# A four-block transformer on one core: softmax scaling moved from VectorE to GpSimd, and decay rows in two row groups

## The chip, the cores and the metric

One core of a Trainium2 chip. The time is device microseconds of one execution, the median of three runs; lower is better. Everything is in float32. TensorE's granted clock has two levels, 2.4 and 1.2 GHz; the profile gives it as a share of the higher one (PEclk).

## What is computed

A sequence of 256 tokens, 1024 wide, goes through a first block (an HGRN/RG-LRU mixer and a feed-forward; then a forgetting attention, "fox", and a feed-forward) and a second block (latent attention, "mla", and a feed-forward; then an S5 state-space mixer and a mixture of eight experts). The change lies in the two attentions, cut here to what matters:

```
def fox_attention(q, k, v, f_logit):                    # 16 heads of 64
    c = cumsum(log_sigmoid(f_logit), axis=1)            # one decay row of 256 per head
    for blk in range(2):                                # query blocks of 128
        logits = einsum('bhqd,bhkd->bhqk', q[blk] * 64**-0.5, k[:end])
        logits = logits + c[q] - c[k]
        p = softmax(where(causal, logits, -inf))
        out[blk] = einsum('bhqk,bhkd->bhqd', p, v[:end])

def mla_mixer(...):                                     # 16 heads of 64, and 32 rotary dimensions
    s = einsum(q_nope, k_nope) + einsum(q_pe, k_pe)
    p = softmax(where(causal, s * scale, NEG_INF))
    o = einsum(p, v)
```

The term `c[q]` is the same for a whole softmax row and falls out, so the kernel adds only `-c[k]`.

## The kernel before, in words

Each engine has a program of its own, in a fixed order written out by hand; the engines meet at semaphores. Both attentions run through `attention(kind, ...)`, which exists once for TensorE (L1309), once for ScalarE (L641) and once for VectorE (L1983). The 16 heads go in 8 pairs. A head has 384 columns of scores in one PSUM bank: query block 0 against keys 0 to 127, then query block 1 against keys 0 to 255. Banks 4 to 7 hold two pairs.

For pair p, TensorE does, in this order:

- `scores(p + 2)`: the products q·k of two heads (`head_products`, L1377; a head has 64 partitions, 0 to 63 or 64 to 127); then in mla the rotary products (L1458; 32 partitions, at 32 times the head's number modulo 4), and in fox the decay rows (L1422: a column of the identity, broadcast, times `negc`, 16 partitions by 384 columns, one matmul per head); then the causal mask (L1332). A float32 matmul stands in the profile as two.
- `output(p - 1)`: probabilities times values (L1353).
- `turn(2p)`, `turn(2p + 1)`: six transposes of probabilities (L1341). Each head's wait for `at["prob"]`.

ScalarE takes the exponentials with their row sums (L649, L652), writes the mask into a freed bank (`biased`, L659), copies the turned probabilities of the even head to SBUF (L667) and the pair's output (L672).

VectorE takes the maxima (`maximum`, L1989 to L1993), copies the odd head's turned probabilities (`turned`, L2009), and normalizes (`normalize`, L1995): a reciprocal of the two row sums (L1998), then the two scalings of `pbuf` in place, 128 and 256 columns (L1999, L2001). Its order in the loop over pairs is

```
maximum(2 * p + 2)
maximum(2 * p + 3)
if p:
    turned(p - 1)
normalize(2 * p)
normalize(2 * p + 1)
```

so that in the last two pairs, which have no maxima left, a reciprocal and its scalings come straight after a copy. `negc` is made once, in VectorE's `fox` (L2050 on), from `cum`, on partitions 0 to 15.

GpSimd has two memsets at the start (L506, L507), a causal select in the first mixer (L510), and the three pieces of `mask3` (L515, L516), which it writes at 130 us. After that its program is at its end.

Of the kernel before, what the change touches and what calls it, by code (L numbers as in the profile page):

```python
# [14 lines left out]
P = 128  # L15
T = 256
# [149 lines left out]
def build_program(nc, a):  # L166

    ctx = ExitStack()
    with ctx:
# [86 lines left out]
        def pair(f, k):  # L256
# [38 lines left out]
            "rate", "conv", "product", "gates", "decay", "square", "root")}  # L295
        at = {n: sem("at_" + n) for n in (
            "flog", "maskmade", "biased", "fscaled", "rcol", "rcoltaken", "fbias", "logsig", "c", "vtile", "vtaken", "scores", "max", "exp", "prob",
            "pturned", "eventaken", "oddtaken", "out", "posrow", "poscol", "reduced", "trig", "turned", "roped")}
        s5 = {n: sem("s5_" + n) for n in (
            "dt", "angle", "mag", "trig", "bbar", "bturned", "btaken", "steps", "phase", "sincos",  # L300
            "astep", "cstep", "kcopied", "kernel", "aturned", "ataken", "bu", "rotated", "state", "y", "ysum", "z")}
# [65 lines left out]
        UP0, SCALED0, HID0 = ({name: m * FT0[name] for name in LATE} for m in (2, 1, 1))  # L367

        cum, fz, fa = (scr[0:HEADS, i * T:(i + 1) * T] for i in range(3))
        negc = scr[0:HEADS, 4 * T:4 * T + 3 * P]  # L370
        mraw = part(0, 6).rearrange("p (a n) -> p a n", a=6)
        mnorm = part(6, 5).rearrange("p (a n) -> p a n", a=5)
        qpe_raw = part(12, 4).rearrange("p (a n) -> p a n", a=4)
# [130 lines left out]
        @block.gpsimd  # L504
        def _(pool):
            pool.memset(ones[:, :], 1.0).then_inc(cleared, 1)  # L506
            pool.memset(xbp[:, :, 0:3], 0.0).then_inc(cleared, 1)  # L507

            pool.wait_ge(hg["scopied"], 2)
            pool.affine_select(out=sc, in_=sc, pattern=[[0, 16], [1, CHUNK]], base=0,  # L510
                               channel_multiplier=-1, compare_op=ALU.is_ge, fill=0.0
                               ).then_inc(hg["masked"], 1)
            pool.wait_ge(mix_ready, KD)
            for b in (0, 2):
                pool.tensor_copy(mask3[:, b * P:(b + 1) * P], mask).then_inc(at["maskmade"], 1)  # L515
            pool.memset(mask3[:, P:2 * P], 0.0).then_inc(at["maskmade"], 1)  # L516


        @block.scalar
# [486 lines left out]
        def _(pe):  # L1006
# [310 lines left out]
            def attention(kind, products):  # L1317
                n0 = at0[kind]
                p0 = n0 // 2
                b0 = 0 if kind == "fox" else HEADS // 2 - 2  # L1320

                def scores(p):

                    if p >= 2:
                        pe.wait_ge(at["biased"], b0 + p - 1)
                        pe.wait_ge(at["exp"], n0 + 2 * p - 2)
                    else:
                        pe.matmul(ps[:, 4 + 2 * p, 0:3 * P], ident, mask3, start=True, stop=False,
                                  skip_group_check=True)
                    products((2 * p, 2 * p + 1))  # L1330
                    for c in (0, 2 * P):
                        m = pe.matmul(ps[:, 5 + 2 * p % 4, c:c + P], ident, mask, start=False,  # L1332
                                      stop=True, skip_group_check=True)
                    m.then_inc(at["scores"], 1)

                def turn(h):
                    pe.wait_ge(at["prob"], n0 + h + 1)
                    if h >= 2:
                        pe.wait_ge(at[("eventaken", "oddtaken")[h % 2]], p0 + h // 2)
                    for b in range(3):  # L1340
                        m = pe.transpose(ps[:, 2 + h % 2, b * P:(b + 1) * P],  # L1341
                                         pbuf[h % 4][:, b * P:(b + 1) * P], ident)
                    m.then_inc(at["pturned"], 1)

                def output(p):

                    pe.wait_ge(at["eventaken"], p0 + p + 1)
                    pe.wait_ge(at["oddtaken"], p0 + p + 1)
                    if p >= 2:
                        pe.wait_ge(mix_ready, mix_at[kind] + p - 1)  # L1350
                    for b in range(2):
                        for h in (2 * p, 2 * p + 1):
                            m = pe.matmul(ps[HD * (h % 2):HD * (h % 2) + HD, p % 2, b * P:T],  # L1353
                                          vtok[:, b, h * HD:(h + 1) * HD],
                                          pTs[h % 4][:, 2 * b * P:2 * P + b * P], start=b == 0,
                                          stop=b == 1, skip_group_check=True)
                    m.then_inc(at["out"], 1)

                pe.wait_ge(at["vtaken"], 4 if kind == "fox" else 8)
                pe.wait_ge(at["maskmade"], 3)  # L1360
                scores(0)
                scores(1)
                for p in range(HEADS // 2):
                    if p + 2 < HEADS // 2:
                        scores(p + 2)
                    if p:
                        output(p - 1)
                    turn(2 * p)
                    turn(2 * p + 1)
                output(HEADS // 2 - 1)  # L1370
# [28 lines left out]
            def fox():  # L1399
                linear("odd_qk", hT, h_ready, H0["n4"], range(1))  # L1400
                for c in range(KD):
                    m = pe.matmul(acc(2)[0:HEADS], wf[:, c, :], hT[:, c], start=c == 0,
                                  stop=c == KD - 1, skip_group_check=True)
                m.then_inc(at["flog"], 1)
                presummed_total("n4")
                linear("odd_qk", hT, h_ready, H0["n4"], range(1, 3))
                pe.wait_ge(rstd_ready, NORM_NO["n4"] + 1)
                for g in range(2):
                    pe.matmul(ps[:, 0, g:g + 1], rstd[0:1, g * P:(g + 1) * P], ones[0:1, 0:1],
                              start=True, stop=True, skip_group_check=True).then_inc(at["rcol"], 1)  # L1410
                linear("odd_qk", hT, h_ready, H0["n4"], range(3, 16))
                pe.wait_ge(at["fscaled"], 1)
                pe.wait_ge(at["rcoltaken"], 1)
                values("odd_v", hT, KD, 0)
                pe.wait_ge(tile_taken, TILE0["odd_qk"] + 16)
                pe.wait_ge(at["c"], 2)

                def products(heads):
                    head_products(heads)
                    for h in heads:  # L1420
                        one = cst[0:HEADS, CST["ident"] + h:CST["ident"] + h + 1]
                        m = pe.matmul(ps[:, 4 + h % 4, 0:3 * P], one.to_broadcast([HEADS, P]), negc,  # L1422
                                      start=False, stop=h % 2 == 0, skip_group_check=True)
                        if h % 2 == 0:
                            m.then_inc(at["scores"], 1)

                attention("fox", products)

            def mla():
# [3 lines left out]
                busy(2, 3)  # L1433
                total("mq")

                pe.wait_ge(at["posrow"], 2)
                pe.matmul(acc(2), onesrow, posf, start=True, stop=True, skip_group_check=True
                          ).then_inc(at["poscol"], 1)
                total("mkv", 3)
                busy(6, 3)  # L1440
                linear("mla_uq", mnorm, h_ready, H0["mq"])
# [391 lines left out]
        def _(dve):  # L1833
# [149 lines left out]
            def attention(kind):  # L1983
# [9 lines left out]
                    dve.tensor_scalar(stat[:, h, 3:5], stat[:, h, 0:2], -scale_of[kind], None,  # L1993
                                      ALU.mult).then_inc(at["max"], 1)

                def normalize(h):
                    dve.wait_ge(at["exp"], n0 + h + 1)
                    step(dve.reciprocal(stat[:, h, 7:9], stat[:, h, 5:7]))  # L1998
                    dve.tensor_scalar(pbuf[h % 4][:, 0:P], pbuf[h % 4][:, 0:P], stat[:, h, 7:8],  # L1999
                                      None, ALU.mult)  # L2000
                    dve.tensor_scalar(pbuf[h % 4][:, P:3 * P], pbuf[h % 4][:, P:3 * P],  # L2001
                                      stat[:, h, 8:9], None, ALU.mult).then_inc(at["prob"], 1)

                def turned(p):

# [8 lines left out]
                for p in range(HEADS // 2):  # L2014
                    if p + 1 < HEADS // 2:
                        maximum(2 * p + 2)
                        maximum(2 * p + 3)
                    if p:
                        turned(p - 1)
                    normalize(2 * p)  # L2020
                    normalize(2 * p + 1)
                turned(HEADS // 2 - 1)

            def fox():
# [13 lines left out]
                for i in range(1, 3):  # L2038
# [8 lines left out]
                dve.tensor_tensor_scan(cum, one.to_broadcast([HEADS, T]), fz, 0.0, ALU.mult, ALU.add  # L2047
                                       ).then_inc(at["c"], 1)
                dve.wait_ge(at["c"], 1)
                dve.tensor_scalar(negc[:, 0:P], cum[:, 0:P], -1.0, None, ALU.mult)  # L2050
                dve.tensor_scalar(negc[:, P:3 * P], cum, -1.0, None, ALU.mult
                                  ).then_inc(at["c"], 1)
                for i in range(4, 16):
                    take_tile(i)
                attention("fox")
# [242 lines left out]
            def mla():  # L2298
# [6 lines left out]
                                      ).then_inc(tile_taken, 1)  # L2305
                dve.wait_ge(tile_taken, TILE0["mla_in"] + 6)
                dve.wait_ge(late_loaded, 16 * 4)
                dve.tensor_copy(posf, pos_i[:, :]).then_inc(at["posrow"], 1)
                dve.memset(onesrow, 1.0).then_inc(at["posrow"], 1)
                pre_norm("mq", mraw, mnorm, "q_norm", 0)  # L2310

                dve.wait_ge(at["poscol"], 1)
                step(dve.tensor_scalar(ang, acc(2), v("inv_freq", 0), None, ALU.mult))
                reduce_angle(red, ang, turns).then_inc(at["reduced"], 1)
                pre_norm("mkv", mraw[:, 3:5], mnorm[:, 3:5], "kv_norm", 0)
# [467 lines left out]
```

## Time and profile before

| | |
|---|---|
| three runs | 2281.67, 2281.91, 2285.21 us; median 2281.91 |
| profiled execution, span | 2281.3 us; the page gives no other time of that execution |
| busy in the span | TensorE 2211.3 us (97%), VectorE 871.5 (38%), ScalarE 467.1 (20%), GpSimd 3.3 (0%) |
| mean granted clock | 0.989 |
| fox attention | 489.88 to 530.46 us |
| mla attention | 864.01 to 900.52 us |

Times in the rows are microseconds from the start of the span. Busy time is the time in which an engine executed something; instructions of one engine overlap in part, so a row's length is not its share of the engine, and start-to-start distances are the safer reading. A matmul's end is modelled.

### The profile page before, as it was taken

The numbers are of one execution on the slowest core, as the hardware profiler recorded it, in microseconds if no ns is written. First come the engines' busy times: TensorE is split into PE (matmuls) and PEld (weight loads), VectorE is DVE, ScalarE is ACT, GpSimd is POOL, SyncE is SP. The second block draws the span as 40 slices with busy tenths as digits, with TensorE's granted clock in tenths as the row PEclk, the third lists the DMA queues.
The fourth block names the chain that finished last, engine by engine and source line by source line (L and its number), as shares of the span: only waits on it lengthen the run. The fifth ranks groups of instructions, "written<-read, shape, count | busy, mean of one in ns | idle before, by whom it ended". The sixth has DMA issues, their size and how long they took to land.

```text
span 2281.3 us, 67869 instructions
## 1 busy us (share of the span) xinstructions
PE 2211.3 (97%) x30612; PEld 2019.5 (89%) x30612; DVE 871.5 (38%) x2198; ACT 467.1 (20%) x1074; POOL 3.3 (0%) x10
## 2 busy tenths in 40 slices
PE   9999999999999999999978999999999999999998
PEld 8879998857899876999966899999999999999998
DVE  4257765224766536567678210101010101111101
ACT  3432112123211234110043211111111111111111
POOL 0000000000000000000000000000000000000000
PEclk9999999999999999999999999999999999999999
DMA  7142444232144322444322199999999999999996
GB/s 322 74 166 96 155 159 164 92 129 111 70 160 160 134 81 105 190 158 158 119 98 93 56 337 398 330 399 343 393 339 391 353 368 374 359 381 344 390 355 253
DMA packets 103298, 522.45 MB, mean 229 GB/s; under 512 B 8402, under 2 KB 8531, under 8 KB 95443
## 3 DMA queue, kind: packets, MB, share of 16 engines
q1 hardware_dynamic: 103122, 519.82, 59.3%
q8 instruction: 146, 2.39, 0.4%
q14 instruction: 30, 0.24, 0.0%
HBM read 518.74 MB, written 1.05 MB: 228 GB/s over the span
## 4 chain that ended last, share of the span: by engine, by line
PE 61%; DVE 3%; ACT 1%; issue 1%; DVEq 0%; ACTq 0%
PE ps L1731 26%; PE ps L1745 13%; PE ps L1126 6%; PE ps L1159 4%; PE ps L1056 3%; PE ps L1521 2%; PE ps L1718 1%; PE ps L1689 1%; DVE scr L2393 1%; PE ps L1703 0%; PE ps L1391 0%; PE ps L1377 0%; PE ps L1458 0%; PE ps L1504 0%; PE ps L1353 0%
## 5 line engine op out<-in xcount | busy, mean ns | idle before, releaser
L1731 PE MATMUL ps<-scr,slot 128*64 128x96 f32 x14336 | 636.6, 246 | 2.8 <-issue 2.7
L1731 PEld LDWEIGHTS ps<-scr,slot 128*64 128x64 f32 x14336 | 610.9, 137 | 4.0 <-issue 3.7
L1745 PE MATMUL ps<-scr,slot 128*64 128x96 f32 x7168 | 341.3, 247 | 0.0
L1745 PEld LDWEIGHTS ps<-scr,slot 128*64 128x64 f32 x7168 | 313.3, 137 | 24.0 <-issue 24.0
L2522 DVE TENSOR_TENSOR scr<-scr,ps 128x96 f32<-128x96 f32 x224 | 56.5, 252 | 611.8 <-PE ps L1731 611.8
L1159 PE MATMUL ps<-scr,slot 128*128 128x256 f32 x1056 | 244.7, 387 | 7.9 <-DVE scr L2210 7.9
L1159 PEld LDWEIGHTS ps<-scr,slot 128*128 128x128 f32 x1056 | 200.3, 195 | 34.9 <-DVE scr L2210 9.5
L908 ACT ACTIVATE scr<-ps 128x96 f32<-128x96 f32 x224 | 56.1, 250 | 824.9 <-PE ps L1731 824.9
L1126 PE MATMUL ps<-vtok,slot 128*128 128x128 f32 x1056 | 139.8, 276 | 2.7 <-DVE vtok L2150 2.7
L1126 PEld LDWEIGHTS ps<-vtok,slot 128*128 128x128 f32 x1056 | 128.6, 192 | 3.5 <-DVE vtok L2150 3.5
L1126 PE MATMUL ps<-vtok,proj 128*128 128x128 f32 x1056 | 128.7, 275 | 0.0
L1126 PEld LDWEIGHTS ps<-vtok,proj 128*128 128x128 f32 x1056 | 123.2, 192 | 0.0
L1126 PEld LDWEIGHTS ps<-hT,slot 128*128 128x128 f32 x960 | 116.4, 192 | 2.9
L1126 PE MATMUL ps<-hT,slot 128*128 128x128 f32 x960 | 116.9, 275 | 0.0
L1056 PE MATMUL ps<-hT,slot 128*128 128x256 f32 x480 | 111.1, 385 | 3.9 <-issue 1.6
L1056 PEld LDWEIGHTS ps<-hT,slot 128*128 128x128 f32 x480 | 89.1, 190 | 23.4 <-issue 6.7
L2136 DVE TENSOR_TENSOR proj<-slot 128x512 f32<-128x512 f32 x132 | 91.1, 690 | 6.2 <-ACT mixT L672 2.9
L765 ACT ACTIVATE sq<-ps 128x128 f32<-128x128 f32 x66 | 18.3, 277 | 364.4 <-PE ps L1126 364.4
L1208 PE MATMUL ps<-hT,slot 128*128 128x256 f32 x384 | 89.5, 394 | 2.2 <-DMA slot<-in_w_even_in 1.9
L1208 PEld LDWEIGHTS ps<-hT,slot 128*128 128x128 f32 x384 | 75.5, 198 | 14.3 <-DMA slot<-in_w_even_in 2.1
L2160 DVE TENSOR_TENSOR sq<-sq,ps 128x128 f32<-128x128 f32 x66 | 18.9, 287 | 175.4 <-ACT sq L765 175.4
L1056 PE MATMUL ps<-mixT,slot 128*128 128x256 f32 x384 | 84.6, 381 | 1.3 <-PE ps L1056 0.9
(391 smaller groups left out, 2127.3 us busy)
## 6 DMA issues: line engine op xcount, KB each, us to landing
slot<-in_w_moe SPq DMA_DIRECT2D x224, 1024.0 KB, 7.1
slot<-in_w_moe SPq DMA_DIRECT2D x224, 512.0 KB, 6.9
slot<-in_w_ffn SPq DMA_DIRECT2D x33, 3072.0 KB, 10.2
slot<-in_w_even_in SPq DMA_DIRECT2D x3, 3072.0 KB, 27.4
slot<-in_w_odd_qk SPq DMA_DIRECT2D x2, 3072.0 KB, 10.9
slot<-in_w_s_glu SPq DMA_DIRECT2D x2, 3072.0 KB, 11.3
slot<-in_w_odd_v SPq DMA_DIRECT2D x2, 2048.0 KB, 8.2
slot<-in_w_even_in SPq DMA_DIRECT2D x2, 1536.0 KB, 11.8
```

Of the source, the lines that this page charges most:

```text
L908: act.activation(gbuf[j][:, 0:CAP], pair(j, 0)[:, 0:CAP], ACT.Silu).then_inc(gate_act, 1)
L1056: m = pe.matmul(ps[:, bank0 + n % ring, 0:T], w[:, o:o + P], src[:, c], start=c == 0, stop=c == k - 1, skip_group_check=True)
L1126: m = pe.matmul(product(k, n), weights[:, c * P:(c + 1) * P], x[:, c], start=first and c == 0, stop=c == 3, skip_group_check=True)
L1159: m = pe.matmul(acc(d), w[:, o:o + P], hid2[u % 2][:, half], start=u == half == 0 and d % 2 == 0, stop=last, skip_group_check=True)
L1208: m = pe.matmul(even_tile(i), project.w[:, o:o + P], hT[:, c], start=c == 0, stop=c == KD - 1, skip_group_check=True)
L1521: m = pe.matmul(glu_tile(i), w[:, o:o + P], hT[:, c], start=c == 0, stop=c == KD - 1, skip_group_check=True)
L1689: m = pe.matmul(ps[s:s + STRIP, bank0 + b, k * CAP:(k + 1) * CAP], vtok[:, g, c * P + s:c * P + s + STRIP], pick[:, g], start=g == 0, stop ...
L1718: pe.matmul(ps[:, bank, :], place[:, n // 2 * P:n // 2 * P + P], ye[:, n % 2 * 512:n % 2 * 512 + 512], start=True, stop=True, skip_group_c ...
L1731: m = pe.matmul(pair(f, k)[s:s + STRIP, 0:CAP], w[:, o:o + STRIP], xg[e % 2][:, c], start=c == 0, stop=c == KD - 1, skip_group_check=True)
L1745: m = pe.matmul(y_sum(d)[s:s + STRIP], w[:, o:o + STRIP], hid[f % 4][:, 0:CAP], start=f == 0 and d % 5 == 0, stop=f == FE_TILES - 1, skip_ ...
L2136: dve.tensor_tensor(dst, a, b, ALU.subtract).then_inc(combined, 1)
L2522: dve.tensor_tensor(hid[f % 4][:, 0:CAP], gbuf[f % 4][:, 0:CAP], pair(f, 1)[:, 0:CAP], ALU.mult).then_inc(hid_ready, 1)
```

## The change

The two scalings of each head leave VectorE. VectorE now only takes the reciprocal and raises `at["inverse"]`; GpSimd waits for it, scales `pbuf` in place and raises `at["prob"]` twice per head, for which `turn` waits. In fox, VectorE writes `negc` twice, to partitions 0 to 15 and to partitions 32 to 47, and the decay matmul of an odd head reads the second copy, with a column of the identity from the same partitions. Two semaphores of the mla prologue are merged into others.

```
-        negc = scr[0:HEADS, 4 * T:4 * T + 3 * P]
+        negc = [scr[r:r + HEADS, 4 * T:4 * T + 3 * P] for r in (0, ROPE)]
...
+            def probabilities(kind):
+                for h in range(HEADS):
+                    pool.wait_ge(at["inverse"], at0[kind] + h + 1)
+                    pool.tensor_scalar(pbuf[h % 4][:, 0:P], pbuf[h % 4][:, 0:P], stat[:, h, 7:8],
+                                       None, ALU.mult).then_inc(at["prob"], 1)
+                    pool.tensor_scalar(pbuf[h % 4][:, P:3 * P], pbuf[h % 4][:, P:3 * P],
+                                       stat[:, h, 8:9], None, ALU.mult).then_inc(at["prob"], 1)
+            probabilities("fox")
+            probabilities("mla")
...
-                    pe.wait_ge(at["prob"], n0 + h + 1)
+                    pe.wait_ge(at["prob"], 2 * (n0 + h + 1))
...
-                        one = cst[0:HEADS, CST["ident"] + h:CST["ident"] + h + 1]
-                        m = pe.matmul(ps[:, 4 + h % 4, 0:3 * P], one.to_broadcast([HEADS, P]), negc,
+                        r = h % 2 * ROPE
+                        one = cst[r:r + HEADS, CST["ident"] + r + h:CST["ident"] + r + h + 1]
+                        m = pe.matmul(ps[:, 4 + h % 4, 0:3 * P], one.to_broadcast([HEADS, P]), negc[h % 2],
...
-                def normalize(h):
+                def invert(h):
                     dve.wait_ge(at["exp"], n0 + h + 1)
-                    step(dve.reciprocal(stat[:, h, 7:9], stat[:, h, 5:7]))
-                    dve.tensor_scalar(pbuf[h % 4][:, 0:P], pbuf[h % 4][:, 0:P], stat[:, h, 7:8],
-                                      None, ALU.mult)
-                    dve.tensor_scalar(pbuf[h % 4][:, P:3 * P], pbuf[h % 4][:, P:3 * P],
-                                      stat[:, h, 8:9], None, ALU.mult).then_inc(at["prob"], 1)
+                    dve.reciprocal(stat[:, h, 7:9], stat[:, h, 5:7]).then_inc(at["inverse"], 1)
...
-                dve.tensor_scalar(negc[:, 0:P], cum[:, 0:P], -1.0, None, ALU.mult)
-                dve.tensor_scalar(negc[:, P:3 * P], cum, -1.0, None, ALU.mult
-                                  ).then_inc(at["c"], 1)
+                for n in range(2):
+                    dve.tensor_scalar(negc[n][:, 0:P], cum[:, 0:P], -1.0, None, ALU.mult
+                                      ).then_inc(at["c"], 1)
+                    dve.tensor_scalar(negc[n][:, P:3 * P], cum, -1.0, None, ALU.mult
+                                      ).then_inc(at["c"], 1)
```

VectorE before, one pair in the middle of an attention (`scr<-scr,stat` is `pbuf` scaled; `scr<-ps` is the copy of the odd head's turned probabilities):

```order
L2009 COPY scr<-ps 128x384 [waits at_pturned]
L1998 RECIPROCAL stat<-stat 128x2 [waits at_exp]
L1999 TENSOR_SCALAR scr<-scr,stat 128x128 [waits dve_own]
L2001 TENSOR_SCALAR scr<-scr,stat 128x256
L1998 RECIPROCAL stat<-stat 128x2 [waits at_exp]
L1999 TENSOR_SCALAR scr<-scr,stat 128x128 [waits dve_own]
L2001 TENSOR_SCALAR scr<-scr,stat 128x256
L1989 TENSOR_REDUCE stat<-ps 128x3 [waits at_scores]
```

VectorE now, the same place (line numbers are those of the changed kernel):

```order
L2018 COPY scr<-ps 128x384 [waits at_pturned]
L2011 RECIPROCAL stat<-stat 128x2 [waits at_exp] x2
L2002 TENSOR_REDUCE stat<-ps 128x3 [waits at_scores]
L2004 TENSOR_TENSOR stat<-stat 128x1 [waits dve_own]
L2006 TENSOR_SCALAR stat<-stat 128x2 [waits dve_own]
```

GpSimd now, behind the mask that it writes at 130 us, the first two of 32 heads:

```order
L516 MEMSET scr 128x128
L522 TENSOR_SCALAR scr<-scr,stat 128x128 [waits at_inverse]
L524 TENSOR_SCALAR scr<-scr,stat 128x256
L522 TENSOR_SCALAR scr<-scr,stat 128x128 [waits at_inverse]
L524 TENSOR_SCALAR scr<-scr,stat 128x256
```

The two reciprocals of a pair now stand side by side on VectorE; the four scalings stand in a row on GpSimd. The order on TensorE and ScalarE is the same as before.

## Rows read from the trace of the kernel before

**Rows 1.** The page, part 1: busy time, share of the span, instructions.
```profile
PE 2211.3 (97%) x30612; PEld 2019.5 (89%) x30612; DVE 871.5 (38%) x2198; ACT 467.1 (20%) x1074; POOL 3.3 (0%) x10
```

**Rows 2.** Windows: the whole fox attention, then the whole mla attention.
```profile
core 0: us, PE busy (x) PEld busy (x) DVE busy (x) ACT busy (x) POOL busy (x), PEclk, DMA share, GB/s
489.88:530.46 40.58, 38.49 (x244) 23.37 (x244) 27.84 (x104) 22.62 (x86) 0.00 (x0) 1.00 0.21 79
864.01:900.52 36.51, 33.54 (x276) 22.25 (x277) 27.21 (x104) 22.44 (x86) 0.00 (x0) 1.00 0.23 88
```

**Rows 3.** Windows: one pair in steady state, mla and then fox.
```profile
882.04:886.00 3.96, 3.96 (x35) 2.69 (x34) 3.39 (x13) 2.76 (x12) 0.00 (x0) 1.00 0.00 0
505.52:510.11 4.59, 4.59 (x32) 2.84 (x31) 3.48 (x13) 2.76 (x12) 0.00 (x0) 1.00 0.00 0
```

**Rows 4.** Timeline of TensorE in fox: start, length, engine, line, out<-in, count.
```profile
506.38 1.55 PE L1422 MATMUL ps<-scr,cst 16*128 16x384 f32 x4
507.86 0.71 PE L1332 MATMUL ps<-cst 128*128 128x128 f32 x4
```

**Rows 5.** Timeline of TensorE in mla, the pair of rows 3.
```profile
882.90 0.92 PE L1458 MATMUL ps<-scr,proj 32*128 32x128 f32 x8
883.75 0.71 PE L1332 MATMUL ps<-cst 128*128 128x128 f32 x4
...
885.20 0.87 PE L1341 MATMUL ps<-cst,scr 128*128 128x128 f32 x6
```

**Rows 6.** Timeline of VectorE in the same pair of mla.
```profile
882.15 0.56 DVE L2009 COPY scr<-ps 128x384 f32<-128x384 f32 x1 [0.36 <-PE ps L1341]
882.63 0.16 DVE L1998 RECIPROCAL stat<-stat 128x2 f32<-128x2 f32 x1
...
883.94 0.55 DVE L1989 TENSOR_REDUCE stat<-ps 128x3 f32<-128x384 f32 x1
884.53 0.16 DVE L1991 TENSOR_TENSOR stat<-stat 128x1 f32<-128x1 f32 x1
```

**Rows 7.** Timeline of the tail of mla: VectorE, and TensorE's loads that waited.
```profile
895.95 0.31 PEld L1341 LDWEIGHTS ps<-cst,scr 128*128 128x128 f32 x3 [0.16 <-DVE scr L2001]
...
896.54 0.56 DVE L2009 COPY scr<-ps 128x384 f32<-128x384 f32 x1 [0.64 <-PE ps L1341]
897.01 0.16 DVE L1998 RECIPROCAL stat<-stat 128x2 f32<-128x2 f32 x1
...
897.21 0.29 DVE L1999 TENSOR_SCALAR scr<-scr,stat 128x128 f32<-128x128 f32 x1
897.41 0.35 DVE L2001 TENSOR_SCALAR scr<-scr,stat 128x256 f32<-128x256 f32 x1
897.67 0.16 DVE L1998 RECIPROCAL stat<-stat 128x2 f32<-128x2 f32 x1
...
898.47 0.20 PEld L1341 LDWEIGHTS ps<-cst,scr 128*128 128x128 f32 x2 [0.16 <-DVE scr L2001]
```

**Rows 8.** Timeline: GpSimd's copies of the mask, beside VectorE.
```profile
130.12 0.42 DVE L1980 TENSOR_TENSOR mixT<-sq,proj 128x256 f32<-128x256 f32 x1
...
130.57 0.69 DVE L2136 TENSOR_TENSOR proj<-slot 128x512 f32<-128x512 f32 x1
130.60 1.54 POOL L515 COPY scr<-cst 128x128 f32<-128x128 f32 x2 [40.68 <-DVE mixT L1980]
131.29 0.69 DVE L2136 TENSOR_TENSOR slot<-slot 128x512 f32<-128x512 f32 x1
```

**Rows 9.** Groups of GpSimd's instructions: busy us, mean ns, idle before and releaser.
```profile
L510 POOL TENSOR_SCALAR_AFFINE_SELECT proj<-proj 64x1024 f32<-64x1024 f32 x1 | 1.1, 1143 | 87.7 <-ACT proj L623 87.7
L506 POOL MEMSET ones<- 128x128 f32 x1 | 0.2, 204 | 0.3 <-POOLq L2774 0.3
L507 POOL MEMSET xbp<- 128x12 f32 x1 | 0.1, 110 | 0.0
```

**Rows 10.** Timeline: VectorE's first maximum in fox.
```profile
492.50 0.56 DVE L1989 TENSOR_REDUCE stat<-ps 128x3 f32<-128x384 f32 x1 [31.53 <-PE ps L1422]
```

**Rows 11.** Windows: the S5 stage, columns as in rows 2.
```profile
1150.00:1250.00 100.00, 76.07 (x1153) 62.32 (x1152) 85.72 (x179) 37.18 (x80) 0.00 (x0) 0.91 0.19 71
```

More of the change, by code:

```diff
@@ L297, in build_program @@
             "flog", "maskmade", "biased", "fscaled", "rcol", "rcoltaken", "fbias", "logsig", "c", "vtile", "vtaken", "scores", "max", "exp", "prob",
-            "pturned", "eventaken", "oddtaken", "out", "posrow", "poscol", "reduced", "trig", "turned", "roped")}
+            "inverse", "pturned", "eventaken", "oddtaken", "out", "reduced", "trig", "turned", "roped")}
         s5 = {n: sem("s5_" + n) for n in (
@@ L1415, in fox @@
                 pe.wait_ge(tile_taken, TILE0["odd_qk"] + 16)
-                pe.wait_ge(at["c"], 2)
+                pe.wait_ge(at["c"], 5)
                 def products(heads):
@@ L1434, in mla @@
                 total("mq")
-                pe.wait_ge(at["posrow"], 2)
+                pe.wait_ge(at["rcoltaken"], 3)
                 pe.matmul(acc(2), onesrow, posf, start=True, stop=True, skip_group_check=True
-                          ).then_inc(at["poscol"], 1)
+                          ).then_inc(at["rcol"], 1)
                 total("mkv", 3)
@@ L2019, in attention @@
                         turned(p - 1)
-                    normalize(2 * p)
-                    normalize(2 * p + 1)
+                    invert(2 * p)
+                    invert(2 * p + 1)
                 turned(HEADS // 2 - 1)
@@ L2307, in mla @@
                 dve.wait_ge(late_loaded, 16 * 4)
-                dve.tensor_copy(posf, pos_i[:, :]).then_inc(at["posrow"], 1)
-                dve.memset(onesrow, 1.0).then_inc(at["posrow"], 1)
+                dve.tensor_copy(posf, pos_i[:, :]).then_inc(at["rcoltaken"], 1)
+                dve.memset(onesrow, 1.0).then_inc(at["rcoltaken"], 1)
                 pre_norm("mq", mraw, mnorm, "q_norm", 0)
-                dve.wait_ge(at["poscol"], 1)
+                dve.wait_ge(at["rcol"], 3)
                 step(dve.tensor_scalar(ang, acc(2), v("inv_freq", 0), None, ALU.mult))
```

## The prediction

> **What bounds the kernel now.** I read the page first: TensorE is busy for 97% of the span [rows 1], so a change pays only where it shortens TensorE's own work or a wait of TensorE. Then the windows of the two attentions [rows 2]: fox takes 40.58 us, mla 36.51, 3.4% of the span together, and TensorE is at the full granted clock in both (PEclk 1.00). Then one pair of each in steady state [rows 3]: TensorE is busy for 3.96 of 3.96 us in mla and 4.59 of 4.59 in fox. It waits for nobody there. VectorE, busy for 3.39 and 3.48 us, is close behind but not ahead. Last, the tail, where no scores are left to fill the gaps: there TensorE's transposes of the odd head begin when VectorE's second scaling ends [rows 7].
>
> **The decay rows.** In fox the four decay matmuls start at 506.38 and the mask follows at 507.86: 1.48 us [rows 4]. Mla has work of the same size at the same place, two heads of 384 columns, on 32 partitions each, at different partitions for the two heads: 882.90 to 883.75, 0.85 us [rows 5]. So matmuls at different partitions run side by side and the decay matmuls, all at partition 0, do not. Put at partitions 0 and 32, a pair should fall from 1.48 to 0.85, 0.63 us less, the difference of the two periods, 4.59 and 3.96 [rows 3]. With that, fox's TensorE program is mla's, length for length, and so is the work of VectorE and ScalarE. Hence I take the whole difference of the two attentions, 40.58 - 36.51 = **4.1 us saved**: six steady pairs of 0.63 are 3.8, the rest lies in the start, where the first exponentials hide most of it. The bounds: nothing saved if 16 partitions do not pair, and 8 x 0.63 = 5.0 if the start gave all of it.
>
> **Work added at no cost.** Two more small scalings for the second `negc`: VectorE had been waiting 31.5 us for TensorE when its first maximum began [rows 10]. Without that cover they would cost under 0.7 us, two of the 0.35 us scalings [rows 7]. The merged semaphores keep their places. GpSimd has had nothing to do since 132 us, and issues no DMA.
>
> **GpSimd's price per head, h**, for 128 and 256 columns. No row shows a scaling on GpSimd. Below: memsets take 110 ns for 12 columns and 204 ns for 128 [rows 9], 0.8 ns a column, so 0.20 and 0.31 us, h = 0.5. Above: two copies of 128 columns took 1.54 us [rows 8]; at 0.8 us an instruction h = 1.6. But each copy began within 0.06 us of a VectorE instruction of 0.69 us and ended only after it. The select's 1024 columns in 1.14 us [rows 9] are 1.0 ns a column over a fixed 0.1. I take 1.0 ns x 384 and two fixed parts of 0.2 (a scaling reads a tensor and a scalar, more than a memset), **h = 0.8**, with 0.5 and 1.6 as ends.
>
> The Trainium skill (GPSIMD Engine Reference, the introduction and "Engine selection") says that the Vector engine is about twice as fast on elementwise work, though one-input operations run at roughly line rate. Twice VectorE's 0.46 us (897.21 to 897.67 [rows 7]) would be h = 0.92, and by the tail sum below the kernel would then gain 1.5 us, not 2.5: 2280.4.
>
> **Steady pairs.** VectorE's first reciprocal ends at 882.79 [rows 6]. GpSimd starts 0.06 us after its releaser (130.54 to 130.60 [rows 8]), at 882.85, and has both heads done 2h later. The odd head's transposes begin about 0.33 us into the group at 885.20 [rows 5]. With 0.05 for the hand-over to TensorE, 2h may be 2.6 us. At h = 0.8 GpSimd needs 1.6, so 1.0 us of slack is left, and nothing is saved either: VectorE's relief of some 0.9 us a pair lies beside a full TensorE.
>
> **The tail.** Two pairs per attention. Before, from the start of VectorE's copy to the odd head's transposes: 896.54 to 898.47, 1.93 us [rows 7]. Now: the reciprocal ends at +0.63, GpSimd starts at +0.69, works 2h, and hands over in 0.05: 0.74 + 2h. The wait grows by 2h - 1.19, at h = 0.8 by 0.41 us. The output of a pair waits for that copy in turn, so it counts fully: 4 x 0.41 = **1.6 us lost** over both attentions.
>
> **Sum:** -4.1 + 1.6 = -2.5 us on the span of 2281.3. The median, 2281.91, lies 0.6 above that span, and I carry the difference over: **2279.4 us**. What is freed passes on, as TensorE is the pace in what follows.
>
> **Rivals.**
>
> *GpSimd becomes the pace.* From the odd head's transposes to the copy is 0.59 us [rows 7], then 0.74 + 2h to the next pair's: a loop of 1.33 + 2h that reaches mla's 3.96 at h = 1.31. At the copies' h = 1.6 it is 4.53: 0.57 us more on up to 12 pairs, 6.8, and the tails lose 4 x 2.01 = 8.0. With the 4.1 saved: +10.7, **2292.6**, slower. For it stand the copies' length; against it what they ran beside. Chance 0.10.
>
> *VectorE and GpSimd hold each other up.* The copies ended 0.15 us behind VectorE's instruction both times [rows 8]. VectorE's maxima have four small instructions per pair that work in SBUF. If each waits for one scaling of 0.5 us, VectorE's pair is 3.96 less 0.4 idle less 0.9 removed plus 2.0, 4.66: 0.7 on 12 pairs, +8, less the 2.5: **2287.4**. It decides from about 0.3 us per wait. Against: GpSimd works from 882.85 to 884.45, and the first of the four stands at 884.53 [rows 6]. Chance 0.05.
> By the Trainium skill (SBUF — State Buffer, "Who interferes with whom") the two share a port pair as an exclusive lock against VectorE instructions with two SBUF inputs; the copies, beside just such instructions, agree.
>
> *The decay rows do not pair,* since no row shows 16 partitions doing so. Only the tail's 1.6 us is left: **2283.5**. Chance 0.08.
>
> *GpSimd is quick,* h at 0.6 or less: the tail costs nothing and the full 4.1 stay: **2277.8**. Chance 0.17.
>
> **How the numbers follow.** The forecast's own case, h between 0.6 and 1.3, has 0.60. One thing moves all of them: the granted clock is 0.91 over the S5 stage [rows 11], where it falls for short stretches, and the three runs of the same kernel lie 3.5 us apart. I take half of that, 1.7 us, for a stretch more or less. A measurement tells 0.2%, 4.6 us, from no change. Below 2277.3: half of the quick case, and a few hundredths from the clock, 0.14. Above 2286.5: the pace rival, most of the hold-up rival and a little of the clock, 0.15. Within: 0.71. The range reaches from the quick case less one stretch, 2276, to the hold-up rival, 2288.
>
> **What would show it.** In the changed profile: the two heads' decay matmuls start a few ns apart and the mask follows 0.85 us after the first; a fox pair lasts 3.96 us, as mla's does; fox takes about 37.3 us and mla 37.3. GpSimd's four scalings of a pair take 1.6 us from the first start. In the tail, TensorE's loads for the odd head wait for GpSimd, 2.3 us after the copy's start. A mla pair longer than 3.96, with TensorE waiting for GpSimd, would mean that the pace rival holds; VectorE's small instructions in the maxima longer than 0.16 us, the hold-up one.

## The result, and the profile after

The changed kernel takes 2296.37 us (median of 6 runs, 2290.88 to 2300.43), the one before 2281.79 in the same comparison: ratio **1.0059, 95% interval 1.0043 to 1.0075**, some 13 us slower by the ratio. I had forecast 2279.4, with a range from 2276 to 2288. Two executions of the study, one of 5836.73 us (the kernel before) and one of 2869.35 (the kernel with idle matmuls, at a granted clock of 0.75), stand far outside all others and are left out of the ratios.

The page of the changed kernel, part 1, which answers to [rows 1], and the first line of the chain that ended last, here and then in the kernel before:

```profile
PE 2218.1 (96%) x30612; PEld 2020.5 (88%) x30612; DVE 857.0 (37%) x2136; ACT 467.0 (20%) x1074; POOL 50.9 (2%) x74
...
PE 59%; DVE 3%; POOL 1%; issue 1%; ACT 1%; POOLq 0%; DVEq 0%
...
PE 61%; DVE 3%; ACT 1%; issue 1%; DVEq 0%; ACTq 0%
```

GpSimd went from 3.3 to 50.9 us of work, and it stands in the chain that sets the end, where it had no share. VectorE lost only 14.5 us. The windows of fox, then mla, in the changed kernel, as in [rows 2]:

```profile
core 0: us, PE busy (x) PEld busy (x) DVE busy (x) ACT busy (x) POOL busy (x), PEclk, DMA share, GB/s
492.46:539.75 47.29, 40.59 (x244) 23.77 (x244) 20.21 (x72) 22.42 (x86) 23.84 (x32) 0.84 0.17 68
871.41:915.37 43.96, 36.39 (x276) 22.77 (x276) 20.24 (x72) 22.54 (x86) 23.83 (x32) 0.94 0.19 73
```

Fox grew from 40.58 to 47.29 us and mla from 36.51 to 43.96: 14.2 us together, near the 14.6 us between the medians. The profiled executions themselves lie 17.3 us apart (spans 2298.6 and 2281.3), and single executions of one kernel differ by as much as 15 us, so the agreement is in part luck: the parts are told below. The granted clock, 1.00 in both before, is 0.84 and 0.94. GpSimd's 32 instructions take 23.8 us per attention, 1.49 us per head. Its groups by form in the changed kernel, beside [rows 9]:

```profile
L524 POOL TENSOR_SCALAR scr<-scr,stat 128x256 f32<-128x256 f32 x32 | 29.5, 922 | 0.0
L522 POOL TENSOR_SCALAR scr<-scr,stat 128x128 f32<-128x128 f32 x32 | 19.3, 602 | 731.3 <-DVE stat L2011 731.3
L515 POOL COPY scr<-cst 128x128 f32<-128x128 f32 x2 | 1.5, 797 | 42.3 <-DVE mixT L1993 42.3
```

One loop in the middle of mla, one pair of heads long. First its window of the changed kernel (columns as above):

```profile
891.19:895.53 4.34, 4.17 (x35) 2.67 (x34) 2.58 (x9) 2.75 (x12) 2.98 (x4) 1.00 0.01 4
```

Then its timeline (start in us, mean time of one, engine, line, operation, the wait ahead of it in brackets):

```profile
892.03 0.60 POOL L522 TENSOR_SCALAR scr<-scr,stat 128x128 f32<-128x128 f32 x1 [1.36 <-DVE stat L2011]
892.61 0.92 POOL L524 TENSOR_SCALAR scr<-scr,stat 128x256 f32<-128x256 f32 x1
...
893.51 0.60 POOL L522 TENSOR_SCALAR scr<-scr,stat 128x128 f32<-128x128 f32 x1
893.61 0.28 DVE L2004 TENSOR_TENSOR stat<-stat 128x1 f32<-128x1 f32 x1
...
894.09 0.92 POOL L524 TENSOR_SCALAR scr<-scr,stat 128x256 f32<-128x256 f32 x1
...
895.07 0.31 PEld L1353 LDWEIGHTS ps<-cst,scr 128*128 128x128 f32 x3 [0.40 <-POOL scr L524]
...
895.65 0.56 DVE L2018 COPY scr<-ps 128x384 f32<-128x384 f32 x1 [0.62 <-PE ps L1353]
896.13 0.22 DVE L2011 RECIPROCAL stat<-stat 128x2 f32<-128x2 f32 x2
896.38 0.60 POOL L522 TENSOR_SCALAR scr<-scr,stat 128x128 f32<-128x128 f32 x1 [1.36 <-DVE stat L2011]
```

The window of one pair lasts 4.34 us, not 3.96 [rows 3]. The timeline shows why. Start to start, GpSimd's instructions take 0.58 and 0.90 us, h = 1.48. TensorE's loads wait 0.40 us for the last, then come the transposes, VectorE's copy at 895.65, the reciprocals, and GpSimd starts again at 896.38, 4.35 us after 892.03. Yet GpSimd is idle for 1.36 us of each pair: it isn't full, it sits in a loop. The tail of mla, timeline of the same kernel:

```profile
908.10 0.31 PEld L1353 LDWEIGHTS ps<-cst,scr 128*128 128x128 f32 x3 [1.17 <-POOL scr L524]
...
908.69 0.56 DVE L2018 COPY scr<-ps 128x384 f32<-128x384 f32 x1 [3.65 <-PE ps L1353]
909.16 0.22 DVE L2011 RECIPROCAL stat<-stat 128x2 f32<-128x2 f32 x2
...
912.45 0.50 PEld L1353 LDWEIGHTS ps<-cst,scr 128*128 128x128 f32 x3 [0.98 <-POOL scr L524]
```

From the copy at 908.69 to the odd head's loads at 912.45 are 3.76 us, where 1.93 stood before [rows 7]. The loads of 0.50 us instead of 0.31 in the last row run at the lower clock. The windows from there to the end of mla, and just behind it:

```profile
911.00:915.37 4.37, 3.09 (x14) 1.82 (x14) 0.56 (x1) 0.77 (x2) 1.39 (x2) 0.50 0.03 6
915.37:920.00 4.63, 4.63 (x20) 3.86 (x18) 3.82 (x6) 0.38 (x1) 0.00 (x0) 0.79 0.00 0
```

The clock is at its lower level, 1.2 GHz, once TensorE has waited for GpSimd through the tail, and it stays there a little past the window. An estimate from the second row: 0.21 x 4.63, some 1.0 us lost behind mla, which the attention windows don't count.

The decay rows did what they should. TensorE in a fox pair of the changed kernel, timeline, beside [rows 4]:

```profile
512.08 0.91 PE L1435 MATMUL ps<-scr,cst 16*128 16x384 f32 x4
512.93 0.71 PE L1344 MATMUL ps<-cst 128*128 128x128 f32 x4
```

0.85 us in place of 1.48.

### The profile page after: what moved, and what is told of

Same layout as the page of the kernel before. It is cut to its first block, busy times and chain, and to the rows that moved or that the text cites. A ratio compares the mean times of both kernels' runs of the same rounds, so it can differ in the third digit from the quotient of the medians.

```text
span 2298.6 us, 67871 instructions
## 1 busy us (share of the span) xinstructions
PE 2218.1 (96%) x30612; PEld 2020.5 (88%) x30612; DVE 857.0 (37%) x2136; ACT 467.0 (20%) x1074; POOL 50.9 (2%) x74
## 4 chain that ended last, share of the span: by engine, by line
PE 59%; DVE 3%; POOL 1%; issue 1%; ACT 1%; POOLq 0%; DVEq 0%
PE ps L1744 26%; PE ps L1758 13%; PE ps L1138 6%; PE ps L1171 4%; PE ps L1068 4%; PE ps L1534 2%; PE ps L1731 1%; PE ps L1702 1%; DVE scr L2404 1%; POOL scr L524 1%; POOL scr L522 0%; PE ps L1716 0%; PE ps L1403 0%; PE ps L1517 0%; PE ps L1033 0%
## 5 line engine op out<-in xcount | busy, mean ns | idle before, releaser
L1068 PEld LDWEIGHTS ps<-mixT,slot 128*128 128x128 f32 x384 | 73.7, 194 | 13.9 <-issue 3.4
```

The source lines that it names most:

```text
L1068: m = pe.matmul(ps[:, bank0 + n % ring, 0:T], w[:, o:o + P], src[:, c], start=c == 0, stop=c == k - 1, skip_group_check=True)
```

## The experiments

Two theories. **Pace and tail:** GpSimd's 1.48 us per head is the whole loss, through the loop and through the tail; the decay rows are a gain. **Against it:** the lowered clock, or the decay rows, or a mutual hold-up with VectorE carries much of it. Stage lengths are windows from the first mask matmul to the last output, as in [rows 2]. Eleven runs were made, of nine kernels; two kernels ran twice.

### Row groups alone

The two copies of `negc` and the matmuls that read them stay; normalizing goes back to VectorE.

```
-        negc = scr[0:HEADS, 4 * T:4 * T + 3 * P]
+        negc = [scr[r:r + HEADS, 4 * T:4 * T + 3 * P] for r in (0, ROPE)]
...
```

> The decay rows in two row groups, alone; VectorE scales as before. Pace theory (GpSimd costs 1.48 us per head and is the whole loss): fox falls to mla's 36.3 us, mla stays at 36.3, TensorE's clock stays full in both attentions, the kernel is 4.1 us faster than before, 2277.7. Rival (pairing the decay rows brings TensorE to wait or lowers its clock, and part of the loss is theirs): fox stays above 38 us or shows a lowered clock, and the kernel is at 2281 or above.

Measured: ratio 0.9979 (0.9964 to 0.9993), median 2276.36 against 2280.38. The same kernel beside the last ones of the study:

> The kernel with row groups alone, a second time, since single executions of one kernel lie up to 15 us apart. If its gain is real, the ratio is again below 1, about 0.998, the mla attention takes 36.3 us, and fox takes 36.3 us in an execution whose clock stays full there and about 4 us more where it falls near fox's start. If the first ratio was chance, this one is 1.000 or above.

Measured: 0.9970 (0.9958 to 0.9981), 2276.67 against 2281.91. So this half of the change gains 5 to 7 us, and is faster than the kernel before and the changed one. The windows of the second execution, fox and mla:

```profile
489.61:530.75 41.14, 38.17 (x244) 23.20 (x244) 27.63 (x104) 22.43 (x86) 0.00 (x0) 0.88 0.20 78
861.34:897.84 36.50, 33.54 (x276) 22.23 (x276) 27.20 (x104) 22.43 (x86) 0.00 (x0) 1.00 0.22 88
```

Mla is untouched. Fox is not at the 36.3 I expected but at 41.14, with a clock of 0.88 (41.10 and 0.88 in the first profile), although GpSimd has no part in it: a fall of the clock near fox's start does not need GpSimd. It is what the rival named, a lowered clock, though the runs are below the rival's 2281. Each profiled execution took longer than the other eleven of its kernel (2280.28 and 2279.49 us), so these fox windows don't show what the half gains in most executions.

### GpSimd alone

```
-                        r = h % 2 * ROPE
-                        one = cst[r:r + HEADS, CST["ident"] + r + h:CST["ident"] + r + h + 1]
-                        m = pe.matmul(ps[:, 4 + h % 4, 0:3 * P], one.to_broadcast([HEADS, P]), negc[h % 2],
+                        one = cst[0:HEADS, CST["ident"] + h:CST["ident"] + h + 1]
+                        m = pe.matmul(ps[:, 4 + h % 4, 0:3 * P], one.to_broadcast([HEADS, P]), negc[0],
```

> Scaling by GpSimd, alone; all decay rows are read from partitions 0 to 15 as before. Pace theory: a fox pair in the middle is TensorE's own 4.59 us, since GpSimd's loop of 4.3 is shorter; only the tails grow, by 1.8 us for each of two pairs, so fox is 44 us plus what a lowered clock adds; mla is 43.8 as in the changed kernel; the kernel takes about 2293 plus the clock's part, 2293 to 2297. Rival (the loss is mostly the clock's, by chance of where the work lies): fox and mla both under 40 us wherever the clock is full.

Measured: 1.0073 (1.0049 to 1.0098), 2297.0 us. The windows of fox, mla and one later pair of fox:

```profile
483.36:531.11 47.75, 42.44 (x244) 25.25 (x244) 20.80 (x72) 22.72 (x86) 23.84 (x32) 0.90 0.18 67
866.83:910.79 43.96, 37.07 (x276) 23.07 (x276) 20.25 (x72) 22.54 (x86) 23.83 (x32) 0.92 0.19 73
506.32:510.91 4.59, 4.59 (x32) 2.84 (x33) 2.65 (x10) 2.76 (x12) 2.98 (x4) 1.00 0.00 0
```

The forecast held, at its upper end: a later fox pair is TensorE's own 4.59. The rival speaks of attentions at a full clock, and there is none here; the kernel with idle matmuls, below, answers it. By the runs alone this kernel and the changed one can't be told apart, as their intervals overlap.

### GpSimd in fox, VectorE in mla

For mla the reciprocal is followed by VectorE's scalings, as in the kernel before.

```
-            probabilities("mla")
...
+                    if kind == "fox":
...
+                        return
...
```

> The changed kernel, but mla's scalings are back on VectorE. Pace theory: fox as in the changed kernel, 44 to 47 us, mla back at 36.3 us with a full clock, so 7.4 us less than the changed kernel: about 2289. Rival (mla's loss comes from the place in time or from the clock, not from GpSimd): mla stays above 38 us.

Measured: 1.0019 (1.0003 to 1.0035), 2285.2 us, a little under the 2289 expected. Its windows of fox and mla:

```profile
486.55:530.51 43.96, 36.98 (x244) 21.26 (x244) 20.32 (x72) 22.53 (x86) 23.84 (x32) 0.93 0.19 73
866.08:902.58 36.50, 33.54 (x276) 22.24 (x276) 27.20 (x104) 22.43 (x86) 0.00 (x0) 1.00 0.23 88
```

Mla is back at 36.50, so its 7.5 us were GpSimd's. Fox, the same instructions as in the changed kernel, takes 43.96, there 47.29: this profile has no clock fall near fox's start, that one has. One such fall is worth 3.3 us here. So the 14.2 us of the changed kernel's windows are twice 7.5 for GpSimd, less the 4.1 of the decay rows, plus 3.3 for this fall.

### Keeping TensorE busy in its waits

```
+                    for _ in range((6 if h >= HEADS - 4 else 0) if h % 2 else (1 if h >= 2 else 0)):
+                        pe.matmul(ps[:, 2 + h % 2, 0:P], ident, mask, start=True, stop=True,
+                                  skip_group_check=True)
                     pe.wait_ge(at["prob"], 2 * (n0 + h + 1))
```

> The changed kernel, with idle matmuls of 128 columns on TensorE before it waits for GpSimd: one per pair, and six before each odd head of the last two pairs; their results are overwritten. If the lowered clock is a consequence of TensorE's waits: the granted clock stays at 1.00 in both attentions, fox falls from 47.1 to about 43.5 us, mla stays near 43.5, the kernel gains 3 to 4 us on the changed one. If the clock falls there for another reason, fox stays at 47. In both cases GpSimd's pace, 4.34 us a pair, stays, which parts the two prices.

Measured: 1.0039 (1.0022 to 1.0057), 2290.63 us. The windows of fox and mla:

```profile
485.17:528.97 43.80, 39.34 (x283) 24.98 (x283) 20.34 (x72) 22.57 (x86) 23.88 (x32) 1.00 0.19 73
859.55:903.36 43.81, 39.40 (x314) 26.76 (x314) 20.27 (x72) 22.57 (x86) 23.88 (x32) 1.00 0.19 73
```

The clock stayed at 1.00 and both attentions still take 43.8, against the rival of the run before last, under 40 wherever the clock is full: pace and tail are not the clock's doing. Nor are they the whole 43.8, as the idle matmuls cost something themselves: a middle pair of mla lasts 4.41 us, not the expected 4.34. The two ratios, 0.002 apart, put the clock's share of the changed kernel near 4.5 us, but their intervals overlap a little. In this profile, the only one of the kernel, idle work kept the clock up in both tails; it hardly touches the 7.4 us.

### GpSimd's price by itself

Ten instructions of each of three kinds are added to the kernel before, on GpSimd alone in the moe stage: a copy, a scaling by 2.0 and a scaling by a column of ones, six of 128 and four of 256 columns each.

```
+            pool.wait_ge(up_ready, 2 * FT0["moe"] + 24)
...
```

> The kernel before, with 30 more instructions on GpSimd in the expert stage, where GpSimd has nothing else to do and VectorE has little: copies, scalings by a constant and scalings by a column, of 128 and 256 columns, each form in two rounds. Theory (GpSimd's scaling has this price by itself): by start-to-start distance a scaling by a column takes 0.58 us for 128 and 0.90 us for 256 columns here too. Rival (the price came from VectorE working beside it, or from the attention's place): 0.40 us or less for 128. For copies both expect 0.2 to 0.3 us, far from the 0.77 of the mask's copies.

GpSimd's groups by form in it (the rows by `ones` are those with a column as the factor):

```profile
L527 POOL TENSOR_SCALAR xbp<-cst,ones 128x256 f32<-128x256 f32 x4 | 3.6, 922 | 0.0
L527 POOL TENSOR_SCALAR xbp<-cst,ones 128x128 f32<-128x128 f32 x6 | 3.6, 602 | 0.2
L527 POOL TENSOR_SCALAR xbp<-cst 128x256 f32<-128x256 f32 x4 | 3.3, 850 | 0.0
L527 POOL TENSOR_SCALAR xbp<-cst 128x128 f32<-128x128 f32 x6 | 3.1, 529 | 0.2
L525 POOL COPY xbp<-cst 128x128 f32<-128x128 f32 x6 | 1.6, 293 | 1229.0 <-PE ps L1744 1229.0
L525 POOL COPY xbp<-cst 128x256 f32<-128x256 f32 x4 | 1.5, 400 | 0.0
```

To the nanosecond the 602 and 922 of the attentions: the price is the instruction's own, not the place's. (It is one run, used for these lengths alone, not for its time.) A scaling costs 2.5 ns a column, a copy 0.8; a column as the factor adds 0.07 us over a constant. The mask's copies of 0.8 us [rows 8] were indeed held up: alone they take 0.29.

### Another price: 128 columns on GpSimd, 256 on VectorE

```
-                    pool.tensor_scalar(pbuf[h % 4][:, P:3 * P], ...).then_inc(at["prob"], 1)
...
+                    dve.tensor_scalar(pbuf[h % 4][:, P:3 * P], pbuf[h % 4][:, P:3 * P],
+                                      stat[:, h, 8:9], None, ALU.mult).then_inc(at["prob2"], 1)
```

> GpSimd scales only the 128 columns of each head, VectorE the 256; decay rows in two row groups. The loop and tail formulas with h = 0.58 in place of 1.48: loop 2.5 us, far below TensorE's 3.96; tail 1.90 us from the copy against 1.93 before. So both attentions at 36.3 us, apart from a lowered clock at fox's start, and the kernel within 1 us of the one with row groups alone. Rival (VectorE's scalings of 256 columns and GpSimd's hold each other up): scalings on VectorE longer than 0.35 us, mla at 37 to 38.5 us.

Measured: 1.0013 (0.9999 to 1.0027), 2283.02 us, worse than expected. Middle pairs 3.96 us, as the loop formula has it. But mla's window:

```profile
857.58:894.74 37.16, 33.83 (x276) 22.21 (x276) 24.46 (x88) 22.46 (x86) 11.84 (x16) 1.00 0.22 86
```

And the timeline of one pair in it, VectorE and GpSimd:

```profile
891.11 0.35 DVE L2012 TENSOR_SCALAR scr<-scr,stat 128x256 f32<-128x256 f32 x1
891.16 1.48 POOL L522 TENSOR_SCALAR scr<-scr,stat 128x128 f32<-128x128 f32 x2 [1.36 <-DVE stat L2010]
```

The two scalings of 128 columns take 1.48 us from 891.16, where 1.18 is their price (0.58, then 0.60 to its end); VectorE's scaling of 0.35 us had begun 0.05 us earlier. The first of the two by itself:

```profile
891.16 0.90 POOL L522 TENSOR_SCALAR scr<-scr,stat 128x128 f32<-128x128 f32 x1 [1.36 <-DVE stat L2010]
```

It takes 0.90 us in place of 0.60; the 0.30 more is what was left of VectorE's scaling when it began. The mean of such a scaling is 750 ns in this kernel, 602 in the changed one. Here a hold-up is real, though it runs the other way from the rival's: GpSimd waits for VectorE, whose own scalings stay at 0.35. It costs the tails 0.3 us a pair and mla 0.66 us. The rest of the distance to the row-group kernel is not explained.

### Pace without tail: the last four heads on VectorE

```
-                for h in range(HEADS):
+                for h in range(HEADS - 4):
...
```

For the other four VectorE does the reciprocal and both scalings, as in the kernel before.

> The changed kernel, but the last four heads of each attention are scaled by VectorE. If the loss has two parts, pace and tail: the middle pairs stay at 4.34 us, the last two are back to 2.4 and 2.5, each attention takes 38.9 us, TensorE's clock does not fall in the tails, and the kernel is 5 us above the one with row groups alone, some 2281 to 2282. If it is all tail, mla is back at 36.3.

The windows of fox and mla:

```profile
489.38:528.83 39.45, 34.77 (x244) 20.31 (x245) 22.57 (x80) 22.57 (x86) 17.92 (x24) 1.00 0.21 81
860.88:900.35 39.47, 34.86 (x277) 22.10 (x277) 22.51 (x80) 22.57 (x86) 17.92 (x24) 1.00 0.21 81
```

Mla 39.47: the pace costs 39.47 - 36.50 = 3.0 us per attention, the tail 43.96 - 39.47 = 4.5, its lowered clock included, and in this profile the clock holds without GpSimd in the tail. The runs say 1.0032 (1.0013 to 1.0051), 2289.34 us, above the 2282 expected. The profiled execution took 2283.18. The three executions with a mean granted clock of 0.991 or more took 2279.07 to 2283.18 us, the seven with 0.989 or less 2289.20 to 2293.48: what puts the median above the forecast goes with a lower clock in a place that this profile doesn't show.

### The loop cut: reciprocals ahead of the copy

```
+                    invert(2 * p)
+                    invert(2 * p + 1)
                     if p:
                         turned(p - 1)
-                    invert(2 * p)
-                    invert(2 * p + 1)
```

> The changed kernel with one exchange in VectorE's order: the reciprocals of a pair stand ahead of the copy of the turned probabilities, not behind it. GpSimd's price per head stays 1.48 us. If the pace came from the loop copy, reciprocal, GpSimd, transposes: it is broken, GpSimd's own 2.96 us per pair fits into 3.96, the middle pairs fall from 4.34 to 3.96, the tail loses about 1.4 us in place of 4.9, mla takes about 38.7 us and the kernel about 2281. If GpSimd itself is too slow, the pairs stay at 4.34.

The window of mla:

```profile
861.79:900.57 38.78, 33.91 (x276) 22.20 (x277) 19.40 (x72) 22.57 (x86) 23.86 (x32) 1.00 0.21 83
```

GpSimd's first scaling of two middle pairs, one after the other, in the timeline:

```profile
880.64 0.60 POOL L522 TENSOR_SCALAR scr<-scr,stat 128x128 f32<-128x128 f32 x1 [0.93 <-DVE stat L2011]
...
884.61 0.60 POOL L522 TENSOR_SCALAR scr<-scr,stat 128x128 f32<-128x128 f32 x1 [0.98 <-DVE stat L2011]
```

GpSimd works as long as ever (23.86 us, 606 and 926 ns), yet the middle pairs are at 3.96 us and mla falls by 5.2 us. So it was the loop through the copy, not a full GpSimd. The runs: 1.0022 (1.0004 to 1.0040), 2285.06 us, 4 us above the forecast, and once more with

> The changed kernel with the reciprocals ahead of the copy, a second time: its profile showed both attentions at 38.5 us, 4.5 us over the kernel with row groups alone, while its runs' median lay 8 to 9 us over that kernel's. If the profile tells the truth, the two ratios of this call are 0.002 apart (4.5 us); if something outside the attentions is slower, 0.004.

1.0006 (0.9991 to 1.0021). Beside 0.9970 in the same call that is 0.0036, near the second of the two cases, though the intervals reach the first. Clock falls outside the attentions stand in every profile of the study, that of the kernel before included ([rows 11]), so they don't settle it. What this kernel loses beyond its attention windows, near 4 us by the medians' ratio, stays open.

### Idle matmuls at the start of the row-group kernel

```
+                    if p == 2:
+                        for _ in range(3):
+                            pe.matmul(ps[:, 2, 0:P], ident, mask, start=True, stop=True,
...
```

> Row groups alone, and three idle matmuls of 128 columns on TensorE before the third pair's scores in each attention, where TensorE waits 0.9 us for the first exponentials. If the fall of the clock near fox's start comes from that wait: full clock in fox, 36.3 us, and 1 to 4 us less than the kernel with row groups alone. If it comes from something else, the fall can stand here too, and the two kernels are equal; in no case should the matmuls cost more than 0.2 us.

The window of fox:

```profile
487.89:524.31 36.42, 34.12 (x250) 21.11 (x250) 27.20 (x104) 22.43 (x86) 0.00 (x0) 1.00 0.23 88
```

Here is fox at the 36.4 us that the pairing promised, mla's length, at a full clock. But the runs give 0.9985 (0.9972 to 0.9999), 2278.70, no better than without the filling. Two profiles of one and the same kernel, the one with early reciprocals, also differ: 38.71 us at clock 1.00, 42.42 at 0.88. So one profile with a full clock proves nothing about the filling; unsettled.

One rival of the early fall was not tested: the pairing of the decay rows itself. The fall some 8 us into fox stands in five of the ten profiles whose decay rows are in two row groups, with GpSimd's scalings or without them. The two profiles with the attention of the kernel before (its own and the price run) have none, and the one of GpSimd alone has a shorter one, later. That is too few to call it shown, and the two ratios of 0.9979 and 0.9970 include whatever it costs.

## Why the prediction was wrong, point by point

- **The decay rows: right.** 1.48 to 0.85 us as forecast, and 36.42 us for fox at full clock (in the kernel with idle matmuls at the start), 4.2 less than before; forecast 4.1. By runs the half alone gains 5 to 7 us.
- **Work at no cost: right** for the second `negc`: in the changed kernel VectorE's first maximum in fox had again waited 31.53 us for TensorE, as in [rows 10].
- **GpSimd's price per head: this step failed.** I took h = 0.8 from the select's 1.0 ns a column and a guess at the fixed parts, and set aside the copies, which I rightly read as held up. The scaling costs 2.5 ns a column: h = 1.48. Two terms hang on it. The steady pairs, which I put at nothing because 1.0 us of slack was left, lost 0.38 us each, 3.0 per attention with the start; the tail, 0.8 per attention in the forecast, cost 4.5. The rows of a select, a memset and a copy were no guide to a multiplication on this engine. The upper end, 1.6, was near, but for a wrong reason, and I gave it 0.10 and left its time out of the range.
- **The Trainium skill** (GPSIMD Engine Reference, "Engine selection") has one-input work at roughly line rate. The copies, 0.8 ns a column, may be that; the scaling by a constant, one input as well, takes three times as much, 2.5. Its other figure, twice VectorE's time, is too low as well: 1.48 against 0.46 us is 3.2 times. The measurement decides.
- **The pace rival: what happened.** Its loop, 1.33 + 2h, gives 4.29 us at 1.48; measured 4.34. Its tail, 2h - 1.19, gives 1.77 a pair; measured 3.76 - 1.93 = 1.83. In sum I would have had 2.0 + 3.5 = 5.5 us per attention and got 7.5. VectorE's copies in mla's timelines show where. From start to start they stand 3.55, four times 3.96, 2.51 and 2.52 us apart before; in the changed kernel six times 4.34, then 4.69. The first comes 0.58 us later in the attention, and the end 0.53 us later behind the last. So the start costs 0.58 + 0.79 = 1.4, four rounds of the loop 1.5, the tail 1.84 + 2.17 + 0.53 = 4.5. What the formula lacks is the start, 0.9 us more than its rounds give, where TensorE waits for GpSimd in the first pair already, and the lower clock in the last pair, also some 0.9 (0.35 and 0.53). With h = 1.48 it would have given -4.1 + 11.0, 2288.8, still 7.6 us short: knowing the price alone would not have been enough.
- **The clock: under-rated.** I allowed one stretch of 1.7 us either way. The clock fell in all five tails where GpSimd does both scalings of the last heads behind the copy (the changed kernel and GpSimd alone, fox and mla; GpSimd in fox only, fox), and in no other tail, those with idle matmuls in the waits included. That TensorE's waits bring it down fits this and is not shown beyond it. The fall near fox's start comes and goes with or without GpSimd.
- **The hold-up rival** was not the cause here: VectorE's small instructions in the maxima did grow beside GpSimd, from 0.16 to 0.28 us in the pair shown (the longest to 0.44), the sign that I had named for it; but they lie inside slack, as the middle pairs of 3.96 us with early reciprocals show. A hold-up of GpSimd by VectorE showed its price in the split kernel.

## What to carry to other kernels

Price an operation on GpSimd by that operation; by the column a copy there is three times too cheap as a guide for arithmetic, and so is a memset of 128 columns as a whole (0.20 against 0.60 us). Work moved to a slower engine is paid where a loop or a tail runs through it, even when the engine is idle a third of the time: count the loop from its own output back to its own input, and take off the loop what doesn't depend on it. A change of two halves should be timed in halves: here one gained about 0.25% and the other lost about 0.7%.

## What the runs showed of the hardware

- GpSimd, float32, 128 partitions: copy 293 ns for 128 columns and 400 for 256; scaling by a constant 529 and 850; by a column 602 and 922.
- A GpSimd scaling that starts 0.05 us behind a VectorE scaling of 256 columns takes 0.90 us in place of 0.60; VectorE's is not longer, 0.35.
- Matmuls of 16 partitions at partitions 0 and 32 run side by side, two heads in 0.85 us against 1.48 with both at 0.
- The same code reached fox's start at 483.4 to 492.5 us in the profiles of these kernels (in that of the changed one at 492.46, of the one before at 489.88). A single profile is compared stage by stage, not by its span.
